# A two-layer transformer kernel on one core: every loop written out, and the weight units sent round their four slots in one global order

## The reference

```python
def first_block(x, ...):
    h = rmsnorm(x, norm_mix_g)
    q, k, v, xr, gr, g_attn, g_rnn = split(h @ w_in)
    attn_out = diff_attention(q, k, v, ...)             # 8 heads
    rnn_out = rg_lru_branch(xr, gr, ...)                # conv, two gates, a scan over time, gelu
    merged = sigmoid(g_attn) * (attn_out @ w_proj_attn) + sigmoid(g_rnn) * (rnn_out @ w_proj_rnn)
    x = x + merged @ w_out
    return x + square(relu(rmsnorm(x, norm_mlp_g) @ w_up)) @ w_down

def second_block(x, mem, ...):
    h = rms_norm(x, mix_norm_g)
    c_b, c_c, c_u, f_q, f_k, f_v, f_g, s_q, s_k, s_v, gates = split(h @ w_in)
    y_conv = short_conv(c_b, c_c, c_u)
    y_fox = fox_attention(f_q, f_k, f_v, cumsum(log_sigmoid(f_g + f_bias)))   # 8 heads
    y_swa = window_attention(s_q, s_k, s_v, rel_bias, sink)                    # 8 heads
    merged = sum(sigmoid(gates[i]) * (y_i @ w_branch[i]) for i, y_i in enumerate((y_conv, y_fox, y_swa)))
    x = x + merged @ w_mix_out
    x = x + cross_attention(rms_norm(x, ...), rms_norm(mem, ...), w_xq, w_xkv, w_xo)
    x = x + (silu(n @ w_gate) * (n @ w_up)) @ w_down     # n = rms_norm(x, ffn_norm_g)
    return rms_norm(x, final_norm_g)
```

## Time and profile before

| | |
|---|---|
| median of 3 runs | 2279.29 us (2279.01, 2279.29, 2282.69) |
| span of the profiled execution, first to last instruction | 2276.7 us (its own device time is not listed apart) |
| TensorE matmuls busy | 2090.8 us, 92% |
| VectorE busy | 1026.6 us, 45% |
| GpSimd busy | 1214.2 us, 53% |
| ScalarE busy | 494.8 us, 22% |

### The profile page before, as it was taken

One profiled execution on the slowest core, in us unless ns is written; L12 is line 12 of the kernel. 1 busy time (PEld: TensorE's weight loads), 2 busy tenths in 40 slices (PEclk: granted clock), 3 DMA queues, 4 the chain that ended last, 5 costly groups with the idle time before them and its releaser, 6 DMA issues.

```text
span 2276.7 us, 26964 instructions
## 1 busy us (share of the span) xinstructions
PE 2090.8 (92%) x9207; PEld 1657.6 (73%) x9207; DVE 1026.6 (45%) x1445; ACT 494.8 (22%) x991; POOL 1214.2 (53%) x1003
## 2 busy tenths in 40 slices
PE   6499997678999999999799989899999889999997
PEld 4366665567887888888667767688878878888886
DVE  6155555884116412215755564443365455313124
ACT  4144443441002201102123222111022121101012
POOL 2233314547665666666423431367775756767663
PEclk9699997889999999999899988899999999999999
DMA  3412311123332333332311421133343333333321
GB/s 91 136 55 64 100 41 53 52 77 92 93 100 80 98 93 93 99 95 65 93 28 35 104 56 46 42 83 97 105 117 93 91 87 96 97 93 101 94 84 55
DMA packets 347573, 186.26 MB, mean 82 GB/s; under 512 B 14749, under 2 KB 341571, under 8 KB 347508
## 3 DMA queue, kind: packets, MB, share of 16 engines
q1 hardware_dynamic: 343188, 179.60, 27.7%
q10 hardware_dynamic: 4320, 5.77, 0.8%
HBM read 183.18 MB, written 8.45 MB: 84 GB/s over the span
## 4 chain that ended last, share of the span: by engine, by line
PE 79%; DVE 11%; issue 3%; ACT 3%; DMA 2%; POOL 0%; SPq 0%; DVEq 0%; ACTq 0%; POOLq 0%
PE bank L628 22%; PE bank L630 22%; PE bank L632 22%; PE bank L746 3%; PE bank L723 2%; DMA RAW<-in_w_in 1%; DMA bias_tiles_l<-bias_rows_l 1%; PE bank L712 1%; PE bank L694 1%; PE bank L778 1%; DVE HS L1687 1%; DVE HS L1686 1%; DVE XC L1657 1%; PE bank L934 1%; DVE GT L1681 1%
## 5 line engine op out<-in xcount | busy, mean ns | idle before, releaser
L595 POOL TENSOR_TENSOR WL<-RAW,WH 128x1024 fp32r<-128x1024 f32 (+3 forms) x331 | 807.5, 2439 | 27.7
L628 PE MATMUL bank<-HH,WH 128*128 128x512 f32 x1560 | 636.1, 408 | 81.8 <-DVE GT L1549 41.9
L632 PE MATMUL bank<-HH,WL 128*128 128x512 f32 x1560 | 628.8, 403 | 0.0
L630 PE MATMUL bank<-HL,WH 128*128 128x512 f32 x1560 | 626.4, 402 | 0.0
L591 POOL TENSOR_TENSOR gate<-gate 128x1 f32<-128x1 f32 x331 | 80.2, 242 | 1004.2 <-PE bank L632 933.3
L628 PEld LDWEIGHTS bank<-HH,WH 128*128 128x128 f32 x1560 | 303.0, 194 | 152.4 <-issue 54.4
L630 PEld LDWEIGHTS bank<-HL,WH 128*128 128x128 f32 x1560 | 303.1, 194 | 62.1 <-issue 3.1
L632 PEld LDWEIGHTS bank<-HH,WL 128*128 128x128 f32 x1560 | 301.9, 194 | 63.0 <-issue 1.7
L592 POOL TENSOR_SCALAR WH<-RAW 128x1024 fp32r<-128x1024 f32 (+3 forms) x331 | 341.0, 1030 | 0.0
L1722 DVE TENSOR_TENSOR X<-X,bank 128x512 f32<-128x512 f32 x80 | 55.0, 687 | 217.3 <-PE bank L632 217.3
L1549 DVE TENSOR_TENSOR GA<-bank,RSTD 128x512 f32<-128x512 f32 x40 | 27.6, 691 | 222.2 <-PE bank L632 222.0
(11 more groups left out here) (396 smaller groups left out, 3279.4 us busy)
## 6 DMA issues: line engine op xcount, KB each, us to landing
RAW<-in_w_in SPq DMA_DIRECT2D x107, 512.0 KB, 3.8
RAW<-in_w_up SPq DMA_DIRECT2D x32, 512.0 KB, 4.0
RAW<-in_w_down SPq DMA_DIRECT2D x32, 512.0 KB, 3.7
RAW<-in_w_ffn_gate SPq DMA_DIRECT2D x22, 512.0 KB, 3.8
RAW<-in_w_ffn_up SPq DMA_DIRECT2D x22, 512.0 KB, 3.9
RAW<-in_w_xkv SPq DMA_DIRECT2D x16, 512.0 KB, 3.9
RAW<-in_w_ffn_down SPq DMA_DIRECT2D x16, 512.0 KB, 4.0
RAW<-in_w_proj_attn SPq DMA_DIRECT2D x8, 512.0 KB, 3.6
```

The source lines that it names most:

```text
L595: nc.gpsimd.tensor_tensor(WL[:, s, 0:k, :], RAW[:, s, 0:k, :], WH[:, s, 0:k, :].bitcast(F32), ALU.subtract).then_inc(S_[f"unit_cut{s}"], 1)
L628: mm(psum[s][:, 0:n], WH[:, s, k, :], hi(k), start=(k == 0), stop=False)
L630: mm(psum[s][:, 0:n], WH[:, s, k, :], lo(k), start=False, stop=False)
L632: last = mm(psum[s][:, 0:n], WL[:, s, k, :], hi(k), start=False, stop=(k == tiles - 1))
```

## The change

Three edits. (1) Every `Fori` on every engine becomes a Python loop, so each iteration is written out as instructions of its own, with constant wait values and constant addresses. (2) The slot of a unit is no longer chosen by phase: the units of the whole kernel are numbered from 0, and unit n uses slot n mod 4. (3) Since the first unit of head 1 now uses bank 3, TensorE waits for `lam_taken` ahead of head 0, for VectorE to have read three small results out of that bank.

```diff
 PHASES = [
-    ("qkv", HEADS, [0, 1, 2], [8, 8, 8]),
+    ("qkv", HEADS, [8, 8, 8]),
...
-    ("merge2", DC, [0, 1, 2, 3, 1], [8, 8, 8, 8, 4]),
+    ("merge2", DC, [8, 8, 8, 8, 4]),
...
     def __init__(self):
...
+        self.place, self.loads_to, self.tiles, self.iters = {}, {}, {}, {}
+        self.order, loads = [], [0] * SLOTS
+        for name, iters, tiles in PHASES:
+            self.tiles[name], self.iters[name] = tiles, iters
+            for it in range(iters):
+                for j in range(len(tiles)):
+                    n = len(self.order)
+                    loads[n % SLOTS] += 1 + ((name, j) in TWO_LOADS)
+                    self.place[name, it, j], self.loads_to[name, it, j] = n, loads[n % SLOTS]
+                    self.order.append((name, it, j))
 
     def use(self, name, it, j):
 
-        slots = self.slots[name]
-        s = slots[j]
-        return s, it * slots.count(s) + self.base[name][s] + slots[:j + 1].count(s)
+        n = self.place[name, it, j]
+        return n % SLOTS, n // SLOTS + 2
...
-            with sp.Fori(1, HEADS) as h:
+            for h in range(1, HEADS):
...
+            for name, it, j in units.order:
+                cut(name, it, j)
...
+            pe.wait_ge(*once("lam_taken"))
...
-            with dve.Fori(0, DC - 1) as n:
-                own.enter(n, 8)
+            for n in range(0, DC - 1):
                 rnn(n, False)
-                own.leave(DC - 1)
```

More of the change, by code:

```diff
@@ L53 @@
 PHASES = [
-    ("qkv", HEADS, [0, 1, 2], [8, 8, 8]),
[L55 to L65, removed]
-    ("merge2", DC, [0, 1, 2, 3, 1], [8, 8, 8, 8, 4]),
[L67 to L71, removed]
+    ("qkv", HEADS, [8, 8, 8]),
+    ("xr0", 1, [8]),
+    ("rnn", DC - 1, [8, 8, 2]),
+    ("rnn_last", 1, [8, 2]),
+    ("merge1", DC, [8, 8, 8, 8]),
+    ("out1", 2, [8] * 4),
+    ("mlp", 4, [8] * 16),
+    ("fgate", 1, [8]),
+    ("fox", 4, [8] * 3),
+    ("swa_first", 1, [8, 8, 8]),
+    ("swa", 3, [8] * 4),
+    ("swa_last", 1, [8] * 3),
+    ("merge2", DC, [8, 8, 8, 8, 4]),
+    ("out2", 2, [8] * 4),
+    ("cross", 4, [8] * 6),
+    ("xout", 2, [8] * 4),
+    ("ffn", 2, [8] * 24),
+    ("ffn_tail", 1, [8] * 12 + [6] * 8),
 ]
@@ L506, in _ @@
             load("fgate", 0, 0, cols(w["w_in_2"], C_FORGET))
-            with sp.Fori(0, 4) as h:
+            for h in range(0, 4):
                 for j in range(3):
@@ L525, in _ @@
             wb = w["w_branch_2"]
-            with sp.Fori(0, DC) as e:
+            for e in range(0, DC):
                 load("merge2", e, 0, cols(wb, e * P))
@@ L828, in _ @@
             rnn_gates(0)
-            with pe.Fori(1, DC - 1) as n:
+            for n in range(1, DC - 1):
                 for j in range(2):
@@ L868, in _ @@
             mlp_group(0, True)
-            with pe.Fori(1, 3) as g:
+            for g in range(1, 3):
                 mlp_group(g)
@@ L926, in _ @@
             pe.wait_ge(S_["f_out_taken"], 9)
-            with pe.Fori(0, DC) as e:
+            for e in range(0, DC):
                 s, c = units.use("merge2", e, 0)
@@ L1239, in _ @@
             squares(0, True)
-            with act.Fori(1, 3) as g:
+            for g in range(1, 3):
                 squares(g, False)
@@ L1292, in fox @@
                 out_hi2("f", YF, h)
-            with act.Fori(0, 3) as h:
+            for h in range(0, 3):
                 fox(h, False)
@@ L1335, in _ @@
             act.preload_act_table(ACT.Sigmoid)
-            with act.Fori(0, DC) as e:
+            for e in range(0, DC):
                 for j in range(3):
@@ L1750, in _ @@
             mlp_group(0)
-            with dve.Fori(1, 3) as g:
+            for g in range(1, 3):
                 mlp_group(g)
@@ L1881, in fox @@
                 take(*following, 2, scaled(M2["VR"][:]))
-            with dve.Fori(0, 3) as h:
-                own.enter(h, 8)
+            for h in range(0, 3):
                 fox(h, False)
-                own.leave(3)
             fox(3, True)
```

93 lines of the change are left out of this document (28 added, 65 removed).

## The result

The changed kernel took 2247.24 us (median of four: 2244.85, 2245.63, 2248.85, 2266.10) beside 2279.15 us before; the ratio is 0.9882, 95% interval 0.9844 to 0.9920. The prediction, 2276.5 us with a range of 2266 to 2287, was wrong: the gain is much larger than the 2.6 us that the sum gave. Measured again beside fifteen runs of before, the same kernel took 2256.77 us (2251.99 to 2258.10), a ratio of 0.9905 (0.9889 to 0.9921). The ten microseconds between the two medians are looked at under after_again.

What follows compares the result with a forecast made beforehand. VectorE, held up by GpSimd's cuts, was taken to bound the recurrent stage, TensorE `merge1`, `merge2` and `ffn`. Terms -9 -6 -1 +13.4 = -2.6 us gave 2276.7, stated as 2276.5 us, range 2266 to 2287.

Steps and rivals of the forecast that it cites:

- head 7 and `fox`: Heads and `fox`: a cut still follows each product's end, so nothing shifts: 0.
- recurrent stage: Recurrent stage: registers -4, chunk 0 -3, chunks 1 to 7 -2, in all -9 us (bounds -20 and +4).
- `mlp` to `fox`: Step from `mlp` to `fox`: `fgate`'s slot frees earlier, VectorE's casts meet fewer cuts, RSTD starts sooner: -6 us.
- `swa`: `swa`: its first unit no longer shares the slot of the unit right ahead, a 0.56 us wait: -1 us.
- `merge2`: `merge2`: unit 4 must wait for VectorE's late read of unit 0's bank, eight steps by 1.67: +13.4 us.
- chunks 1 to 7: Recurrent stage: cuts move against VectorE's operations, held-up time falls slightly: -2 us (bounds -10 to +10 in seven chunks).
- the rival with 0.25: Recurrent stage and `mlp` to `fox`: cuts get out of VectorE's way, about 2265 us; chance 0.25.
- in the other stages with loops: Looped stages other than the recurrent one: TensorE is the bound or waits are for single results, so written-out loops give 0.
- Registers: Recurrent loop, seven chunks: written-out code saves VectorE's register-address cost, 3.5 to 6.3 us, taken as 4.
- Chunk 0: Recurrent stage's first chunk: XR of the next chunk gets another bank, so IT starts 2.5 to 3.7 us sooner: -3.
- The granted clock: `merge2`: rival that the new waits pull down TensorE's clock in each of eight steps, about 2290 us; chance 0.10.
- Straight code fetched too late: Written-out TensorE program: rival that instruction fetches cause 31 waits of 0.6 us, +19 us, 2295; chance 0.05.

Runs made afterwards that it cites:

- after_again: The changed kernel, unaltered, measured and profiled a second time beside the kernel before: 2256.77 us, ratio 0.9905.
- loops_only: The kernel before with all loops written out as in the change, every unit keeping its old slot: 2264.89 us, ratio 0.9942.
- quarters: The changed kernel, with VectorE reading `merge2`'s unit 0 ahead of unit 3 and GpSimd making each WL in four instructions: 2213.26 us, ratio 0.9723.
- both cures: The changed kernel with `merge2`'s unit 4 in unit 1's bank as before, or with VectorE reading unit 0 ahead of unit 3: 2241.56 and 2241.50 us.

## Why the prediction was wrong, point by point

| term | predicted | after | after, again |
|---|---|---|---|
| heads 1-6 | 0 | -1.0 | -0.9 |
| head 7 and `fox` | 0 | -3.2 | +5.9 |
| recurrent stage | -9 | -19.4 | -16.5 |
| `mlp` to `fox` | -6 | -6.1 | -6.1 |
| `swa` | -1 | -8.0 | -0.9 |
| `merge2` | +13.4 | +12.4 | +13.9 |
| memory and cross | 0 | -5.6 | -8.7 |

*The step that failed* is the one on chunks 1 to 7: "the held-up time fell from 5.7 to about 5 us a chunk ... I take -2". In the six chunks from the second to the seventh the hold-ups went from 34.0 us in all to 23.1 (25.8 in the second execution): -10.9 and -8.2, at or beyond the far end of its bound of 10. These chunks took 17.0 and 14.3 us less, and the last one, up to MG, 1.3 less. The mechanism was named rightly, and was the rival with 0.25, though that rival's 2265 was still too high. What was wrong was to believe a layout by hand here: the registers' share alone moves the starting points by 0.8 us a chunk, and in loops_only a chunk of the same program has 3.1 or 7.8 us of hold-up by what the last one left behind.

*The second failed step* is "in the other stages with loops ... I take 0". It priced the loops by their own length. In cross those of TensorE, GpSimd and SyncE moved the cuts by 0.2 us against VectorE, and that gave 5.6 to 8.7 us, though the earlier trace rows showed the 2.35 us wait for XPR that went.

*Registers*: 0.8 us a chunk, 5.6 in seven, predicted 4 with a bound of 6.3; right in kind and engine, low in size. The convolution steps take 2.33 us for three where nothing holds them.

*Chunk 0*: without its hold-up it went from 18.6 to 15.6 us, 2 us beyond the registers (predicted 3), but its hold-up rose from 5.7 to 7.3, so that in all it gave 1.4 us.

*`mlp` to `fox`*: right by place and size in every kernel with the new slots there (-6.0 to -6.1; -7.8 in quarters). *`merge2`*: right; from the first to the last step 12.1 us were added in seven steps, 1.73 each, predicted 1.67, and both cures took it away. The wait is 1.5 us of it, so a stop costs 0.25 us beyond the wait, where 0.13 was put. The granted clock stayed at 1.00 in it, so that rival is out:

```profile
1422.00:1628.00 206.00, 194.21 (x841) 157.05 (x840) 62.92 (x68) 19.60 (x31) 132.07 (x117) 1.00 0.30 83
```

*Straight code fetched too late*: out. The longer waits without a named cause end 0.10 us behind fQL or ROL, so they are waits for VectorE, and the stages of `merge1`, `mlp` and `ffn` kept their lengths to 0.6 us with TensorE's program 1.7 times as long.

*`fox` and `swa`*: predicted 0 and -1. The means over all kernels with these slots are +3.7 and -5.0: two misses that nearly cancel.

*What is chance*: head 7, the first `fox` head and `swa` differ between executions of one program by 3.9, 5.2 and 7.1 us. The first profile had the good side of all three, so a part of the distance from 2276.5 to 2247 is luck. Without them and head 0 the change is worth about 19 us (recurrent 17.9, to `fox` 6.1, cross 7.2, heads 1.0, less `merge2`'s 13.2, all means of the two profiles), from 2277 some 2258 us, and with the two means 2257, near the 2256.8 measured again. Why `swa` varies stays open; it has both cuts that meet VectorE and stretches of low clock, and no kernel here parts them.

## What to carry to other kernels

Where GpSimd and VectorE both work from SBUF, add up how long VectorE's operations take above their clean length: that sum is the stake, and any change that moves either engine by tenths of a microsecond redraws it in all its stages. Such a change is not to be priced by its own terms, and a range for it must take in most of the hold-up time, both ways. Don't tune where the cuts fall: make each GpSimd instruction short, which took another 28 us off here (2241.5 to 2213.3), where GpSimd had the time to spare (54% busy, 64% with quarters).
